# An encoder layer on one core: the output projection forms all left halves first, and the fifth expert's gate and up weights go into the left half of its weights

## What is computed

```
xn = rms_norm(x, norm1_g)
proj = xn @ w_in
x = x + concat([o_gla, o_fnet, o_mla]) @ w_out
x = x + hier_moe(rms_norm(x, norm2_g), ...)
return rms_norm(x, final_norm_g)
```

## Time and profile before

| what | us |
|---|---|
| median of 3 runs | 575.81 (573.13 to 576.08) |
| the profiled execution's own time | 575.18 |
| its span, first to last instruction | 573.4 |
| TensorE busy | 501.1 (87%) |
| VectorE busy | 200.2 (35%) |
| output projection and routing | 226.5 to 312.9 |
| experts, to the last scatter | 312.9 to 547 |

### The profile page before, as it was taken

How to read it: one execution, slowest core, us unless ns; L and a number is a source line. 1 busy time by engine, 2 the same in 40 slices (tenths; PEclk the granted TensorE clock), 3 DMA queues, 4 the chain that set the end, 5 groups by cost and what they waited for, 6 DMA issues and landing times. The chain is left out here.

```text
span 573.4 us, 7727 instructions
## 1 busy us (share of the span) xinstructions
PE 501.1 (87%) x2943; PEld 281.9 (49%) x2943; DVE 200.2 (35%) x496; ACT 144.9 (25%) x334; POOL 99.0 (17%) x116
## 2 busy tenths in 40 slices
PE   4999999997899998999897999999999878897600
PEld 4455544574655665444566755545554443454200
DVE  3227111836476673024864121112112101111257
ACT  4314102426346773011212111111111101110022
POOL 1000002482010000000221123233323222221100
PEclk9999999998979999999997999999999989989955
DMA  8960000100069301910349999999999999999673
GB/s 277 331 178 0 2 1 3 44 0 1 1 228 418 126 1 44 396 68 7 149 162 410 337 402 415 410 413 415 414 414 414 412 412 416 418 415 406 269 294 157
DMA packets 38771, 138.79 MB, mean 242 GB/s; under 512 B 10064, under 2 KB 13008, under 8 KB 30544
## 3 DMA queue, kind: packets, MB, share of 16 engines
q1 hardware_dynamic: 33584, 130.42, 58.0%
q0 software_dynamic: 5056, 7.87, 3.7%
q10 hardware_dynamic: 96, 0.02, 0.0%
HBM read 130.95 MB, written 14.75 MB: 254 GB/s over the span
## 5 line engine op out<-in xcount | busy, mean ns | idle before, releaser
L956 PE MATMUL bank<-EW,WO 128*64 128x256 f32 x640 | 75.2, 389 | 11.9 <-DMA EW<-in_moe_w_up 11.5
L681 PE MATMUL bank<-EW,XT 128*128 128x512 f32 (+1 forms) x192 | 64.1, 495 | 0.0
L956 PEld LDWEIGHTS bank<-EW,WO 128*64 128x64 f32 x640 | 45.0, 139 | 35.9 <-DMA EW<-in_moe_w_up 13.0
L884 PE MATMUL bank<-WO,XT 128*128 128x512 f32 x128 | 58.0, 609 | 1.0 <-DVE XT L1461 1.0
L1215 ACT ACTIVATE G<-bank 128x128 f32<-128x128 f32 x32 | 8.9, 277 | 184.7 <-PE bank L956 184.7
L1557 DVE TENSOR_TENSOR G<-G,bank 128x128 f32<-128x128 f32 x32 | 9.2, 288 | 123.2 <-ACT G L1215 123.2
L681 PEld LDWEIGHTS bank<-EW,XT 128*128 128x128 f32 x192 | 32.9, 190 | 31.0 <-issue 31.0
L1734 POOL DMA_INDIRECT G<-x_scratch,gidx x28 | 28.7, 1024 | 98.7 <-PE bank L946 83.6
L1727 POOL DMA_INDIRECT y_scratch<-G,sidx x32 | 32.5, 1015 | 74.2 <-DVE G L1572 72.2
L1572 DVE COPY G<-bank 128x512 f32<-128x512 f32 x32 | 22.1, 691 | 61.3 <-PE bank L969 53.7
L969 PE MATMUL bank<-EW,G 128*64 128x512 f32 x160 | 38.6, 603 | 0.8 <-issue 0.8
(11 more groups left out here) (254 smaller groups left out, 656.1 us busy)
## 6 DMA issues: line engine op xcount, KB each, us to landing
EW<-in_moe_w_gate SPq DMA_DIRECT2D x20, 1024.0 KB
EW<-in_moe_w_up SPq DMA_DIRECT2D x20, 1024.0 KB
EW<-in_moe_w_down SPq DMA_DIRECT2D x20, 1024.0 KB
WO<-in_w_out SPq DMA_DIRECT2D x2, 2048.0 KB, 12.1
WO<-in_moe_w_gate SPq DMA_DIRECT2D x4, 1024.0 KB
WO<-in_moe_w_up SPq DMA_DIRECT2D x4, 1024.0 KB
WO<-in_moe_w_down SPq DMA_DIRECT2D x4, 1024.0 KB
XT<-in_moe_w_gate SPq DMA_DIRECT2D x4, 1024.0 KB
```

Source lines behind the costliest of these rows:

```text
L681: mm = pe.matmul(ps[:, 0:width], xnT[:, c, t * P:(t + 1) * P], w_in_sb[:, c, col:col + width], start=(c == 0), stop=(c == C - 1))
L884: mm = pe.matmul(ps[:, :], xnT[:, c, t * P:(t + 1) * P], w_out_sb[:, c, n * 512:(n + 1) * 512], start=(c == 0), stop=(c == C - 1))
L956: mm = pe.matmul(bank[BLOCK * m:BLOCK * (m + 1), 0:2 * P].rearrange("p (w n) -> p w n", w=2), xeT[:, buf, c, par * BLOCK:(par + 1) * BLOCK ...
```

## The change

`w_out_sb` is laid out by halves (`[half, chunk, 512]` where it was `[chunk, 1024]`) and loaded by halves in the same two DMAs of 2 MB. The table begins with the left half of all four tiles. The right halves of tiles 1, 2 and 3 are each begun (2 of 8 products, step `begin`) ahead of the steps of the tile before, and finished (6 products) after them. Gate and up of expert 4 go into the left half of `WO`, and are issued as soon as the four left halves are drained, ahead of all scratch stores; down of expert 4 waits as before for the last right half.

```
-OUT_ORDER = [("out", 0, 0), ("out", 0, 1), ("out", 1, 0), ("T", 0), ("norm", 0), ("out", 1, 1), ("Lf", 0),
-             ("out", 2, 0), ("L", 0), ("T", 1), ("norm", 1), ("out", 2, 1), ("Lf", 1), ("pos", 0), ("T", 2), ("norm", 2),
-             ("L", 1), ("out", 3, 0), ("pos", 1), ("Lf", 2), ("L", 2), ("out", 3, 1), ("pos", 2), ("T", 3), ("pick", 0),
-             ("Lf", 3), ("norm", 3), ("L", 3), ("pick", 1), ("pick", 2), ("pos", 3), ("pick", 3)]
+OUT_ORDER = [("out", 0, 0), ("out", 1, 0), ("out", 2, 0), ("out", 3, 0), ("out", 0, 1), ("begin", 1, 1), ("T", 0),
+             ("norm", 0), ("out", 1, 1), ("Lf", 0), ("begin", 2, 1), ("L", 0), ("T", 1), ("norm", 1), ("out", 2, 1),
+             ("Lf", 1), ("pos", 0), ("begin", 3, 1), ("L", 1), ("T", 2), ("norm", 2), ("out", 3, 1), ("Lf", 2), ("T", 3),
+             ("L", 2), ("pos", 1), ("pick", 0), ("Lf", 3), ("norm", 3), ("L", 3), ("pick", 1), ("pos", 2), ("pick", 2),
+             ("pos", 3), ("pick", 3)]
...
-        w_out_sb = view(WO, 0, (C, D))
+        w_out_sb = view(WO, 0, (2, C, 512))
...
-            sp.dma_start(w_out_sb[:, 0:C // 2], w_out_v[:, 0:C // 2]).then_inc(wout_landed, 16)
-            sp.dma_start(w_out_sb[:, C // 2:], w_out_v[:, C // 2:]).then_inc(wout_landed, 16)
+            for n in range(2):
+                sp.dma_start(w_out_sb[:, n], w_out_v[:, :, n * 512:(n + 1) * 512]).then_inc(wout_landed, 16)
...
             for t in range(T):
+                drained(sp, ("out", t, 0))
+            load_gate_up(RING, RING)
+            for t in range(T):
                 if t == T - 1:
-                    for u in range(T):
-                        for n in range(2):
-                            drained(sp, ("out", u, n))
-                    load_gate_up(RING, RING)
+                    drained(sp, ("out", t, 1))
                     load_down(RING, RING)
...
+                    if kind == "begin":
+                        ps, chunks = open_bank(key), range(0, 2)
+                    elif (t, n) in BEGUN:
+                        ps, chunks = banks[PLAN[key][0]], range(2, C)
```

More of the change, by code:

```diff
@@ L144, in psum_plan @@
             late(("x2T", step[1], 1))
-        elif step[0] not in ("pick", "norm"):
+        elif step[0] == "begin":
+            late(("out",) + step[1:])
+        elif step[0] not in ("pick", "norm") and step[1:] not in BEGUN:
             late(step)
@@ L149, in psum_plan @@
     return plan, fills, frees
-OUT_ORDER = [("out", 0, 0), ("out", 0, 1), ("out", 1, 0), ("T", 0), ("norm", 0), ("out", 1, 1), ("Lf", 0),
-             ("out", 2, 0), ("L", 0), ("T", 1), ("norm", 1), ("out", 2, 1), ("Lf", 1), ("pos", 0), ("T", 2), ("norm", 2),
-             ("L", 1), ("out", 3, 0), ("pos", 1), ("Lf", 2), ("L", 2), ("out", 3, 1), ("pos", 2), ("T", 3), ("pick", 0),
-             ("Lf", 3), ("norm", 3), ("L", 3), ("pick", 1), ("pick", 2), ("pos", 3), ("pick", 3)]
+OUT_ORDER = [("out", 0, 0), ("out", 1, 0), ("out", 2, 0), ("out", 3, 0), ("out", 0, 1), ("begin", 1, 1), ("T", 0),
[3 more added lines that the diff above has]
+             ("pos", 3), ("pick", 3)]
+SQUARED = [step[1:] for step in OUT_ORDER if step[0] == "out"]
+BEGUN = [step[1:] for step in OUT_ORDER if step[0] == "begin"]
 def attention_order():
@@ L879, in _ @@
                 kind, t = step[0:2]
-                if kind == "out":
+                if kind in ("out", "begin"):
                     n = step[2]
-                    ps = open_bank(step)
-                    for c in range(C):
-                        mm = pe.matmul(ps[:, :], xnT[:, c, t * P:(t + 1) * P], w_out_sb[:, c, n * 512:(n + 1) * 512],
+                    key = ("out", t, n)
+                    if kind == "begin":
+                        ps, chunks = open_bank(key), range(0, 2)
+                    elif (t, n) in BEGUN:
+                        ps, chunks = banks[PLAN[key][0]], range(2, C)
+                    else:
+                        ps, chunks = open_bank(key), range(0, C)
+                    for c in chunks:
+                        mm = pe.matmul(ps[:, :], xnT[:, c, t * P:(t + 1) * P], w_out_sb[:, n, c, :],
                                        start=(c == 0), stop=(c == C - 1))
-                    close_bank(mm, step)
+                    if kind == "out":
+                        close_bank(mm, key)
                 elif kind == "T":
@@ L1188, in _ @@
                                    scale=float(D) ** -0.5, accum_out=rn2[:, t, 4 * n:4 * n + 1]).then_inc(squares_ready, 1)
-                    act.wait_ge(squares_ready, SQ2 + 2 * t + n + 1)
+                    act.wait_ge(squares_ready, SQ2 + SQUARED.index((t, n)) + 1)
                 elif kind == "norm":
@@ L1490, in _ @@
                     drained(dve, ("out", t, 1))
-                    dve.wait_ge(squares_ready, SQ2 + 2 * t + 2)
+                    dve.wait_ge(squares_ready, SQ2 + SQUARED.index((t, 1)) + 1)
                     dve.tensor_scalar(rn2[:, t, 1:2], rn2[:, t, 0:1], rn2[:, t, 4:5], EPS, ALU.add, ALU.add).then_inc(var_ready, 1)
```

## The result

The changed kernel takes 579.75 us (median of 5, 576.67 to 582.39), the kernel of before 575.81 (median of 5): ratio 1.0071, 95% interval 1.0044 to 1.0098. By the ratio that is 4.1 us slower. The forecast was 580.0, slower.

A forecast was written before the change was run, and what follows sets the result against it. The bound was taken as a fixed-length weight stream from expert 8, timed by expert 0's start. Expert 0 at 314.9 plus 2.4 us of low clock, 317.3 against 312.9, gave +4.4 us: 580 us, 8-in-10 range 574.5 to 583.

The forecast's parts named there:

- The stream's fixed length: From about 324 us, at expert 8's issue, weights stream for a fixed time; each microsecond of expert 0's start is the kernel's.
- The early load is worth 0: Issuing expert 4's gate and up near 257 us only turns 5.1 us of DMA work into idle time; value 0.
- Layout by halves, 0: Loading the projection's weights by halves, in the same two DMAs and 4 MB during attention, costs 0.
- Tile 0 later: Tile 0's first transpose comes later in the projection, so its expert choice L(0) reaches VectorE at about 273.6 us.
- VectorE's chain: During routing VectorE needs 10.0 us a tile against TensorE's 9.4, so TensorE idles 6.7 us before `pick`(2).
- The clock: After TensorE's idle stretch, `pick`(2) and half of `pos`(3) run at the low clock, adding 2.4 us.
- the first rival: The low clock lasts through the stage's end: expert 0 starts 7.7 us later, 583.5 us; chance 0.1.
- The sum: Expert 0 starts at 317.3 us instead of 312.9, +4.4 us, giving a kernel time of 580 us.
- The rival of the absorbed delay: Expert 0's later start is hidden by the weights' queue or a shorter VectorE chain, about 575.5 us; chance together 0.15.
- that of the transfer: Moving 2.1 MB out of the DMA work from 294 us counts in full, 5.1 us earlier, 570.7 us; chance 0.05.
- The fast rival: The last right half ends early and VectorE keeps up, so expert 0 comes earlier, 570.0 us; chance 0.1.

The follow-up runs named there:

- second profile: The changed kernel run again unaltered, profiled in an execution of 579.82 us; ratio to the kernel of before 1.0085.
- filled_gap: The changed kernel with six extra products of no use on TensorE between `pos`(2) and `pick`(2); ratio to the kernel of before 1.0047.
- left_first_short: The changed kernel, its early load and layout kept, with the steps behind the left halves in another order; ratio to the kernel of before 0.9995.
- tiles_short_early: tiles_short with the layout by halves and expert 4's gate and up issued once the four left halves are drained; ratio to the kernel of before 0.9910.
- tiles_short: The kernel of before, its layout, load and order of halves kept, with norms earlier and other steps moved; ratio to the kernel of before 0.9924.
- late_start: The kernel of before with seven chained additions on VectorE between `count` and the reduction that expert 0 waits for; ratio to the kernel of before 1.0145.
- load_back: The changed kernel with gate and up of expert 4 issued where they were before, order and layout still changed; ratio to the kernel of before 1.0077.
- without_2mb: The kernel of before with only 64 of 2048 columns loaded for each of expert 4's gate and up; ratio to the kernel of before 1.0005.
- tiles_short_no_2mb: tiles_short with all but 64 of 2048 columns of expert 4's gate and up left out; ratio to the kernel of before 0.9892.

## Why the prediction was right

By its own steps, against the second profile:

- *The stream's fixed length.* Right for the change. It was 209.5 to 210.5 us in eight of the nine profiles whose issue for expert 8 lay between 321.63 and 329.29. It was 213.9 in the ninth, filled_gap, where the lists held up the loads behind expert 8, and 212.7 and 213.1 in the two where expert 0 came so early that the queue was full at expert 8.
- *The early load is worth 0.* Right, shown two ways: taken back (1.0077) and left out of the kernel of before (1.0005). That it was kept with a shorter order (0.9995) bounds it less closely.
- *Layout by halves, 0.* left_first_short has it at 0.9995, and the stage of tiles_short_early, which has it, is as long as that of tiles_short (71.9 and 71.8), so it costs nothing that shows.
- *Tile 0 later.* L(0) at 273.6 on VectorE, measured 274.14.
- *VectorE's chain.* The last copy ended at 294.0 by my sum and at 294.39; `pick`(2) at 308.1 and at 308.09. TensorE's idle stretch was put at 6.7 us and was 6.48. left_first_short shows that it is the order of these steps that costs.
- *The clock.* 2.4 us put in, about 2.1 by filled_gap and by the rows (3.78 against 2.05, 1.42 against 0.98). The granted clock in the second profile fell in the window at 305 (0.87), was 0.50 when `pick`(2) began and was back at 1.00 in that of 313, so it didn't last through `pick`(3): the first rival did not occur. That it would end so soon was a choice between 1.9 and 5.7; the reason I gave for it, less idle time between the resumed pieces, was never tested, and the two picks at the low clock in left_first_short show that it could have gone on for longer. Here I had some luck.
- *The sum.* Expert 0 at 317.3, measured 316.98; +4.4 us, measured +4.1 in the profile, +3.9 between the medians, +4.1 and +4.9 by the two ratios. The profile flatters the sum a little: the projection began 0.46 us later than before in it, so the stage itself grew by 3.6 us (81.1 against 77.5), 0.8 less than I added up.

The rival of the absorbed delay fell with late_start, that of the transfer with load_back and without_2mb. The fast rival needed VectorE to keep up. TensorE did end the last half early (it went on to `Lf` at 290.34), but VectorE began its add only at 291.75, since the norm of tile 2 stood ahead of it. One thing I didn't forecast: behind expert 1 TensorE now waits for the expert lists, 0.58 us in the second profile and 0.84 in the first. GpSimd's last scatter of list entries ended 1.5 us before expert 0 and now ends 0.6 us after it. The scatter follows `pos`(3) on VectorE by 2.1 us in both profiles (307.06 and 309.18, 313.19 and 315.32); what has changed is that `pick`(3) and `count` behind it now run at full clock and expert 0 follows `pos`(3) by 3.8 us instead of 5.8. Expert 8 is issued before that wait, so it didn't show in the total.

## What to carry to other kernels

Before moving a transfer earlier, look for the last moment at which the queue behind it runs empty: here bytes moved from ahead of that moment turned into idle time, and what started the queue again afterwards was the thing worth making earlier. How far that carries has to be looked up again once it moves: in tiles_short the stage was 5.7 us shorter, and 2.2 of them were lost behind it. When several engines walk one table of steps, add up each engine's work per step: an order that serves the busiest engine can starve it if another engine then gets its work in a lump at the end. And a long wait on TensorE can cost more than itself: what followed the longest waits of this stage ran at half the clock.

## What the runs showed of the hardware

A delay of 5.44 us on TensorE was followed by 3.67 us of matmuls that took 5.53. The same happened around the waits of 2.91 and 6.48 us, and not where the gap was filled with products of no use (2.05 us for `pick` of tile 2 instead of 3.78).

But the waits alone don't say when the clock falls. In tiles_short_no_2mb the waits ahead of `pick`(3) were 1.46, 0.56 and 0.61 us, and in tiles_short_early 1.49, 0.56 and 0.61. There `pick`(3) took 2.05 us and expert 0 3.67; here both ran at the low clock for a part:

```profile
304.16 2.69 PE L918 MATMUL bank<-G,MIX 128*128 128x128 f32 x16 [0.61 <-DVE G L1533]
...
308.74 5.37 PE L958 MATMUL bank<-EW,WO 128*64 128x256 f32 x32 [0.35 <-DVE G L1549]
```

And the last right half took 8.74 us in without_2mb and 7.11 before, with the same waits of 1.2 and 0.4 us ahead of it in both. So a forecast of the low clock is a chance, and one profile doesn't settle it; what decides it no run here shows.

ScalarE's queue loads the expert lists in two transfers of 8 KB, issued from 322.48 in the second profile, which released TensorE at 328.72, 6.2 us later, shortly behind the issue of expert 7's weights. In the same profile a store of a tile of `MIX`, 512 KB, takes 2.7 us from issue to landing (median of 4). So a small transfer on the path to TensorE is not short for being small; that the weights in the queue make it wait is likely, but no run tells it apart.
